# A two-block fp32 layer on one core: C's decays as a fourth score matmul, turned maxima, squares on ScalarE, and softmax visits in halves with other PSUM banks

## What is computed

```python
def forgetting_attention(q, k, v, logf):
    c = jnp.cumsum(logf, axis=1)
    ...
        s = jnp.einsum('bqhd,bkhd->bhqk', qblk, k).astype(jnp.float32) * scale
        decay = jnp.transpose(cblk, (0, 2, 1))[:, :, :, None] - c_k[:, :, None, :]
        s = jnp.where((dist >= 0)[None, None], s + decay, -jnp.inf)
        p = jax.nn.softmax(s, axis=-1)
        return jnp.einsum('bhqk,bkhd->bqhd', p.astype(v.dtype), v)
```

## Time and profile before

| | |
|---|---|
| median of 3 runs | 1279.6 us (1277.46 to 1279.94) |
| the profiled execution | 1279.9 us |
| its span, first to last instruction | 1278.1 us |
| TensorE matmuls busy | 1234.3 us, 97% |
| DVE / ScalarE / GpSimd busy | 658.9 / 550.4 / 659.0 us |
| transfers | 113.94 MB, mean 89 GB/s |
| chain of work that ended last | 83% TensorE, 9% DVE |

### The profile page before, as it was taken

The page is one execution under the profiler, slowest core; times in us unless marked ns, Lnnn a source line. Parts: engine busy times, 40 slices in busy tenths (PEclk is TensorE's granted clock), DMA queues, the critical chain, the costliest instruction groups (busy, mean ns, idle before and its releaser), DMA issues.

```text
span 1278.1 us, 17097 instructions
## 1 busy us (share of the span) xinstructions
PE 1234.3 (97%) x6230; PEld 982.5 (77%) x6230; DVE 658.9 (52%) x1217; ACT 550.4 (43%) x1066; POOL 659.0 (52%) x501
## 2 busy tenths in 40 slices
PE   7998989999999999999989999999999999999996
PEld 5886767777878888888776676878888888888885
DVE  6436744765743312125277545459999999200024
ACT  4544544676654333235552647542332333322344
POOL 4772223235346544446454464646767776655542
PEclk9998999999999999999988999999999999999998
DMA  5333222113222433343231121423333333433321
GB/s 197 112 113 98 67 61 73 50 50 83 67 66 83 114 92 91 95 152 112 82 84 50 42 71 53 116 82 84 99 99 99 90 92 87 128 96 94 100 74 66
DMA packets 63939, 113.94 MB, mean 89 GB/s; under 512 B 7016, under 2 KB 12776, under 8 KB 63856
## 3 DMA queue, kind: packets, MB, share of 16 engines
q1 hardware_dynamic: 63712, 112.84, 31.0%
q10 hardware_dynamic: 144, 0.00, 0.0%
HBM read 110.71 MB, written 2.11 MB: 88 GB/s over the span
## 4 chain that ended last, share of the span: by engine, by line
PE 83%; DVE 9%; ACT 3%; issue 2%; POOL 1%; DMA 1%; DVEq 0%; SPq 0%; ACTq 0%; POOLq 0%
PE pb L911 24%; PE pb L912 24%; PE pb L914 24%; PE pb L1065 2%; PE pb L1041 1%; DVE P L1774 1%; PE pb L1016 1%; POOL HL L2191 1%; DVE B L1644 1%; PE pb L979 1%; DVE U L1644 1%; DVE sq L1632 1%; PE pb L981 1%; PE pb L980 1%; POOL wlo L2191 1%
## 5 line engine op out<-in xcount | busy, mean ns | idle before, releaser
L2191 POOL TENSOR_TENSOR wlo<-raw,whi 128x512 fp32r<-128x512 f32 (+3 forms) x398 | 539.6, 1372 | 437.7 <-ACT whi L1247 437.5
L911 PE MATMUL pb<-HH,whi 128*128 128x512 f32 x968 | 391.4, 404 | 0.0
L912 PE MATMUL pb<-HL,whi 128*128 128x512 f32 x968 | 384.1, 397 | 0.0
L914 PE MATMUL pb<-HH,wlo 128*128 128x512 f32 x968 | 382.6, 395 | 0.0
L1247 ACT ACTIVATE whi<-raw 128x512 fp32r<-128x512 f32 (+3 forms) x398 | 233.2, 613 | 184.5 <-PE pb L914 156.5
L911 PEld LDWEIGHTS pb<-HH,whi 128*128 128x128 f32 x968 | 183.3, 189 | 47.0 <-issue 3.7
L914 PEld LDWEIGHTS pb<-HH,wlo 128*128 128x128 f32 x968 | 182.7, 189 | 42.6
L912 PEld LDWEIGHTS pb<-HL,whi 128*128 128x128 f32 x968 | 182.9, 189 | 42.2 <-issue 2.4
L1644 DVE SCALAR_TENSOR_TENSOR cv<-zf,vecs,cv 128x512 f32<-128x512 f32 x88 | 124.9, 1419 | 3.1
L1322 ACT ACTIVATE P<-P,stat 128x256 f32<-128x256 f32 (+3 forms) x96 | 51.1, 533 | 92.9 <-DVE stat L1639 68.9
L1635 DVE TENSOR_TENSOR X<-pb,X 128x512 f32<-128x512 f32 x24 | 16.6, 691 | 137.7 <-PE pb L914 137.3
(11 more groups left out here) (386 smaller groups left out, 1913.1 us busy)
## 6 DMA issues: line engine op xcount, KB each, us to landing
raw<-in_wall SPq DMA_DIRECT2D x362, 256.0 KB, 2.7
raw<-in_wall SPq DMA_DIRECT2D x16, 192.0 KB, 2.4
raw<-in_wall SPq DMA_DIRECT2D x8, 260.0 KB, 3.1
X<-in_xT SPq DMA_DIRECT2D x8, 256.0 KB, 5.3
N<-c_sums SPq DMA_DIRECT2D x8, 256.0 KB, 4.1
X<-in_xT SPq DMA_DIRECT2D x2, 1024.0 KB, 7.7
outT<-PP SPq DMA_DIRECT2D x8, 256.0 KB, 2.2
raw<-in_wall SPq DMA_DIRECT2D x12, 128.0 KB, 2.1
```

Of the source, the lines that this page charges most:

```text
L911: pe.do.matmul(b, hi, xh[k], start=start, stop=False)
L912: pe.do.matmul(b, hi, xl[k], start=False, stop=False)
L914: m = pe.do.matmul(b, lo, xh[k], start=False, stop=stop)
L2191: g.do.tensor_tensor(lo, x, hi.bitcast(F32), ALU.subtract).then_inc(*up(name, point))
```

## The change

1. C's decay is part of the scores. c and -c are split into high and low parts of 8 rows each (`decay`, in the middle of qC 3), and SP copies the rows one at a time into two operands: AQ with rows c_hi, c_lo, 1, 1 and AK with 1, 1, -c_hi, -c_lo, at partitions 0 to 3 for even heads and 64 to 67 for odd ones. GpSimd sets the ones at the start. `pair` has a fourth matmul over these four rows. The bias is now a constant mask DC; `cq`, the trip through memory and the broadcasts go.
2. The operation that adds the bias also multiplies by -1 and takes the minimum; the exponential has scale -1. C and A need no negation after it; B compares with the negated sink.
3. The squares of x in `first` are made on ScalarE; `lambda` comes after `columns1`; the low parts of odd tiles in `x_norm` are made on DVE.
4. A visit has two halves, after the 4th and the 8th step of a tile (after every step of vA): scores, values, turns and the first normalisation, then the second normalisation and the next biases.
5. Scores and turns have banks 4, 5, 6, 3, 2 (4, 5, 6 during vA as before), projection tiles 0 and 1.

```diff
-        banks = {"main": (0, 1, 2, 3), "first3": (0, 1, 2), "S": (), "Y": (7,), "m3": (0, 1, 2), "x5": (3, 4, 5, 6, 7),
+        banks = {"main": (0, 1, 2, 3), "first2": (0, 1), "S": (), "Y": (7,), "m3": (0, 1, 2), "x5": (3, 4, 5, 6, 7),
                  "x4": (3, 4), "all": (0, 1, 2, 3, 4, 5, 6, 7)}[ring]
         if ring == "S":
             banks = self.score_banks
-        if ring in ("S", "main", "first3"):
+        if ring in ("S", "main", "first2"):
...
-        if i == 7:
+        if i in (3, 7):
             self.step()
...
     def pipeline(self, groups):
 
+
...
-            if 0 < i <= n:
-                for u in groups[i - 1]:
-                    self.add("normal", *u)
...
-            for g in groups[i + 2:i + 4]:
-                for u in g:
-                    self.add("pre", *u)
...
                 self.turns(g)
-            if two:
-                for u in two[0]:
-                    self.add("normal", *u)
+            for u in two[0] if two else ():
+                self.add("normal", *u)
             if kind == "A" and i >= 6 and groups[i - 5][0][2] == 3:
                 h = groups[i - 5][0][1]
                 self.take("S", ("late", h))
                 self.add("late", h)
                 self.ready.add(("yA", h))
+            yield
+            if two:
+                for u in two[1]:
+                    self.add("normal", *u)
+                for g in groups[i + 2:i + 4]:
+                    for u in g:
+                        self.add("pre", *u)
             yield
 
     def turns(self, units):
...
             add("first", k)
             if k <= LOOK:
                 self.split_to(k)
...
-        add("lambda")
...
         add("columns1")
+        add("lambda")
...
-        self.tile("main", ("qC", 3))
+        self.tile("main", ("qC", 3), between=lambda i: add("decay") if i == 4 else None)
         add("out", "qC", 3)
-        take("S", ("cq",))
-        add("cq")
         c, a, b = softmax_units()
         self.background.append(self.pipeline(c))
         add("masks")
-        self.score_banks = (4, 5, 6, 3)
+        self.score_banks = (4, 5, 6, 3, 2)
...
         for k in range(KD):
             self.enter("win", k, VA)
             add("vA", k)
-            if k % 2:
-                self.step()
+            self.step()
...
-        ident, ones, bdones, maskC = (CST[:, 128 * i:128 * i + 128] for i in range(4))
-        DA, DB = CST[:, 512:1024], CST[:, 1024:1280]
+        ident, ones, bdones = (CST[:, 128 * i:128 * i + 128] for i in range(3))
+        DC, DA, DB = CST[:, 384:896], CST[:, 896:1408], CST[:, 1408:1664]
...
+        cum_hi, cum_lo, neg_hi, neg_lo = (like(f"cum{n}", n, dt=F32R)[0:8, :] for n in ("W1", "th1", "W2", "th2"))
+        AQ, AK = (tensor_at(f"decay_{n}", [P, 4 * T], F32R, place[n + "0"]) for n in ("vA", "qB"))
...
-            def forget_columns():
-                free(("cq",))
-                pe.wait_ge(*at("c"))
-                for m in range(4):
-                    i = pe.do.matmul(ps("cq")[:, 8 * m:8 * m + 8], cT[0:8, P * m:P * m + P], ident[0:8, 0:8],
-                                     start=True, stop=True)
-                i.then_inc(*up("small", ("full", ("cq",))))
-
             def pair(one, two):
...
                     for s in range(2):
                         rows = slice(64 * s, 64 * s + 64)
                         z = pe.do.matmul(ps(*tiles[s])[:, 0:wd], qs["q" + kind, t][rows, P * i:P * i + P],
-                                         ks["k" + kind, kt][rows, k0:k0 + wd], start=n == 0, stop=n == 2)
-                        if n == 2:
+                                         ks["k" + kind, kt][rows, k0:k0 + wd], start=n == 0,
+                                         stop=n == 2 and kind == "B")
+                        if n == 2 and kind == "B":
                             z.then_inc(*up("scored", ("full", tiles[s])))
+                if kind == "C":
+                    pe.wait_ge(*at("decay_in"))
+                    for s in range(2):
+                        rows = slice(64 * s, 64 * s + 4)
+                        pe.do.matmul(ps(*tiles[s])[:, 0:wd], AQ[rows, T * t + P * i:T * t + P * i + P],
+                                     AK[rows, T * t:T * t + wd], start=False, stop=True).then_inc(
+                            *up("scored", ("full", tiles[s])))
 
             def scores(kind, h, i):
                 if kind != "A":
...
                 a.do.activation(mh[k], xk[k], ACT.Copy, scale=vecs("norm_gain", k)).then_inc(*up("xhi", ("m_hi", k)))
+                if k > 2:
+                    a.wait_ge(*at("sq_step", k - 2))
+                a.do.activation(sqs[(k - 1) % 2] if k else acc, xk[k], ACT.Square).then_inc(*up("a_norm", ("sq", k)))
...
+            def decay():
+                a.wait_ge(*at("c"))
+                a.do.activation(cum_hi, cT[0:8, :], ACT.Copy).then_inc(*up("a_small", ("cum_hi",)))
+                a.do.activation(neg_hi, cT[0:8, :], ACT.Copy, scale=-1.0).then_inc(*up("a_small", ("neg_hi",)))
...
-                        a.wait_ge(*at("c_minus"))
+                        a.wait_ge(*at("c"))
...
-                    a.do.activation(p, p, ACT.Exp, bias=stat(u, 4 * m + 1), accum_out=stat(u, 4 * m + 2)).then_inc(
+                    a.do.activation(p, p, ACT.Exp, bias=stat(u, 4 * m + 1), scale=-1.0,
+                                    accum_out=stat(u, 4 * m + 2)).then_inc(
...
-                b = sqs[(k - 1) % 2] if k else acc
-                if k > 2:
-                    v.wait_ge(*last("v_sq"))
-                mul(b, xk[k], xk[k], name="v_sq")
-                v.wait_ge(*last("v_sq"))
                 if k:
-                    add(acc, acc, b, *[("sq_sum",)] * (k == KD - 1), name="v_sq")
+                    v.wait_ge(*at("sq", k))
+                    if k > 1:
+                        v.wait_ge(*last("v_sq"))
+                    add(acc, acc, sqs[(k - 1) % 2], ("sq_step", k), *[("sq_sum",)] * (k == KD - 1), name="v_sq")
 
...
+                for n in {2: (1,), 4: (3,), 6: (5,), 7: (7,)}.get(k, ()):
+                    v.wait_ge(*at("x_hi", n))
+                    v.do.tensor_tensor(hl[n], sqs[n % 2], hh[n].bitcast(F32), ALU.subtract).then_inc(
+                        *up("v_lo", ("x_lo", n)))
...
-                v.wait_ge(*last("v_small"))
-                affine(fx, cT[0:8, :], -1.0, None, ALU.mult, None, ("c_minus",))
...
+            def decay():
+                v.wait_ge(*at("cum_hi"))
+                v.wait_ge(*at("c"))
+                v.do.tensor_tensor(cum_lo, cT[0:8, :], cum_hi.bitcast(F32), ALU.subtract).then_inc(
+                    *up("v_lo", ("cum_lo",)))
+                v.wait_ge(*at("neg_hi"))
+                fused(neg_lo, cT[0:8, :], -1.0, neg_hi.bitcast(F32), ALU.mult, ALU.subtract, ("neg_lo",), name="v_lo")
...
             def scores(kind, h, i):
-                u, wd, n = (kind, h, i), width(kind, i), bias_of[kind, h, i]
-                bb = Br[n % 2]
+                u, wd = (kind, h, i), width(kind, i)
                 if kind == "C":
-                    cq = CQ[:, 8 * i + h:8 * i + h + 1]
-                    v.wait_ge(*at("neg", h))
-                    v.wait_ge(*at("cq"))
-                    if n == 0:
-                        v.wait_ge(*at("full", ("qC", 3)))
-                    fused(bb[:, P * i:P * i + P], Nr[h % 4][:, P * i:P * i + P], cq, maskC, ALU.add, ALU.add,
-                          *[("neg_used", h)] * (i == 3), name="v_soft")
-                    if i:
-                        affine(bb[:, 0:P * i], Nr[h % 4][:, 0:P * i], cq, None, ALU.add, None,
-                               *[("neg_used", h)] * (i == 3), name="v_soft")
-                    v.wait_ge(*last("v_soft"))
-                    bias = bb[:, 0:wd]
+                    bias = DC[:, 384 - P * i:512]
                 else:
+                    n = bias_of[kind, h, i]
                     v.wait_ge(*at("bias", n))
-                    bias = bb[:, 384 - P * i:512] if kind == "A" else bb[:, 256 - wd:256]
+                    bias = Br[n % 2][:, 384 - P * i:512] if kind == "A" else Br[n % 2][:, 256 - wd:256]
                 for m in range(2 if kind == "A" else 1):
                     s = soft[(*u, m)]
                     if s >= 6:
                         v.wait_ge(*at("p_used", s - 6))
                     v.wait_ge(*at("full", ("scores", *u, m)))
-                    v.do.tensor_tensor_reduce(Pr[s % 6][:, 0:wd], ps("scores", *u, m)[:, 0:wd], bias, 1.0, LOWEST,
-                                              ALU.add, ALU.max, stat(u, 4 * m)).then_inc(
-                        *up("v_soft", ("empty", ("scores", *u, m))))
-                    v.wait_ge(*last("v_soft"))
+                    most = ("most", u, m)
+                    v.do.tensor_tensor_reduce(Pr[s % 6][:, 0:wd], ps("scores", *u, m)[:, 0:wd], bias, -1.0, -LOWEST,
+                                              ALU.add, ALU.min, stat(u, 0 if kind == "B" else 4 * m + 1)).then_inc(
```

(43 more changed lines are left out.)

37 lines of the change are left out of this document (16 added, 21 removed).

## The result

The changed kernel takes 1284.3 us (median of 5 runs, 1282.6 to 1284.8), the kernel before 1278.9 (5 runs, 1277.5 to 1279.9). The ratio is 1.0040, 95% interval 1.0025 to 1.0054: **slower by 0.4%**, where 1274.9 us was forecast and 1262 to 1283 was the range. The profiled execution took 1284.8 us with a span of 1283.0, so it stands 4.9 us of span above the one before (1278.1).

The account below looks back on a forecast made before the run. TensorE, busy for 97% of the span, was taken as the bound. Gains of -23.6 us and costs of +18.6 gave -5.0 against the profiled 1279.9: 1274.9 us forecast, range 1262 to 1283.

Parts of the forecast that it names:

- C's waits: TensorE's 14 waits in C's stage, 12.8 us, go except two in the visit during vA: -10.7 us.
- four small issues in a row take 1.78 us, 0.445 each: SP's queue: 32 single-row DMAs at this pace, the last leaving at 102.9, stall TensorE by +11.8 us.
- Rival (e): SP's 32 transfers hold one another up; at 0.8 us apiece 1285.9 us, slower from about 0.6; chance 0.07.
- the start: Up to norm1: lambda behind `columns1` and squares on ScalarE remove TensorE's lost time, net -4.9 us.
- Rival (b): The start isn't gained: squares delay ScalarE's splits until TensorE waits as before; 1279.8 us, chance 0.09.
- the odd x_lo: Four low parts go from GpSimd to DVE where TensorE waits for neither: 0 us.
- cq: The `cq` matmuls, which take TensorE from 84.82 to 85.90, go: -1.1 us.
- the old low clock: After TensorE's longest wait, half of 3.85 us at the lower clock until 115.3 is no longer lost: -1.9 us.
- The fourth matmul: C's visits: sixteen pairs stream for 2.5 us, three shape changes in each of 8 visits cost 2.4: +4.9 us.
- The low clock: Behind the new stall at the first four-row matmul the clock drops as after the earlier long wait: +1.9 us.
- A and B: TensorE's waits in the stages of A and B go: -4.3 and -0.7 us.
- Two projection banks: Projection tiles in two banks: one is needed again only after another tile of 5.6 us and a visit: 0 us.

Follow-up runs that it names:

- the run with two queues: Changed kernel with its 32 single-row DMAs kept, AK's 16 issued by ScalarE and AQ's 16 by SP: 1272.5 us, ratio 0.9957.
- the execution with eight DMAs: Changed kernel with AQ and AK filled by 8 DMAs of four rows into one, instead of 32 of one row: 1265.3 us, ratio 0.9887.
- the run with 64 rows: Kernel with 8 DMAs, its fourth matmul contracting over 64 rows (AQ zero beyond its four), memsets at norm1: 1262.5 us, ratio 0.9871.
- the one with the maxima turned back: Kernel with 8 DMAs, but maximum, wait, negation as before the change, in all three stages: 1267.6 us, ratio 0.9919.
- the third set: Third of three sets of follow-up runs, each comparing kernels with the kernel before on the same chip; its median there 1278.1 us.

## Why the prediction was wrong, step by step

The main mechanism was right: an exchange of C's waits against one stall behind SP's queue. Two steps failed. The time is 9.9 us of span above the sum; they make 5.3 and 4.4 of it, and neither alone would have left the range.

**The first step that failed is "four small issues in a row take 1.78 us, 0.445 each".** The rows from which it came are DMAs out of memory, of one row to 128 partitions; the new ones go out of SBUF into a single partition and cost 0.63 an issue, with one source row or four. Which of the two differences makes it dearer no run separates (out of SBUF into memory, -c took one issue of 0.35 in the kernel before). So the last issue leaves at 108.7 and not 102.9, 5.8 us later; the landing took 0.8 less than the 2.6 assumed, TensorE was there 0.3 sooner, and the stall is 17.1 for 11.8. Rival (e) named the point, 0.6 us apiece, from which the kernel is slower than before, and it was passed; its cause, transfers that hold one another up, is ruled out by the run with two queues. With the measured stall in its place the prediction's own sum gives 1280.2: most of what is missing from there is the second step.

**The second is the start**, which was to bring 4.9 and keep it. It brought 4.3 at norm1 (5.5 in the execution with eight DMAs, whose start is the same), and 0.5 at the first sums matmul. The prediction followed TensorE's gain no further than norm1: it had no term for what stands behind x_norm in ScalarE's program, vC's evictions, whose pace did not change. Rival (b) has nearly the size, but not the cause: no wait for ScalarE's splits came back. That the odd x_lo cost nothing was right, by the run that undid them.

**cq**: -1.1 predicted; kA's first tile comes 1.5 us earlier where the first sums matmul came 0.5 earlier, so -1.1.

**C's waits** -10.7, **the old low clock** -1.9: between kA's first tile and the first visit of A, at the same place in the order of projections, the changed kernel loses 12.0 us. Stall 17.1, clock 2.1 and the fourth matmul 6.4 are 25.6; so the waits and the old low clock gave 13.6 where 12.6 were forecast. Right in sum, though this is a remainder and not a measurement, and not by the reason given first: the fifth bank did little of it, so the agreement is in part luck.

**The fourth matmul** +4.9: 6.4. The streaming of 2.5 was right (in the run with 64 rows a pair is followed after 0.11 to 0.12 us at 128 and 256 columns, 0.17 at 384 and 0.24 at 512). The changes of shape cost 3.9 over the eight visits, not 2.4: 0.12 at four places of each, where 0.10 at three was forecast. The rows had changes between 128 and 64 only, and the change back to 128 was taken as no dearer than before. The Trainium skill (TensorEngine Tiling (Array Packing), Key Properties) says that a change of tiling mode drains TensorE. The trace fits that, at 0.24 us for the two sides of one pair.

**The low clock** behind the stall +1.9: 2.1. Right. In the execution with eight DMAs it comes after 2.1 us of waiting as well.

**A and B** -5.0: the visits between the first of A and the end of attention give 5.5 (the changed kernel is 10.5 us behind at the first visit of A, 5.0 at the end of attention, each at the same place among the projections). Right. Two projection banks at 0: right, for no wait on one appears.

The sum by what was measured: -0.5 - 1.1 + 12.0 - 5.5 = +4.9, as in the spans (where 5.0 was forecast the other way: 9.9 apart = 5.3 for the stall, 4.4 for the start, 1.5 for the fourth matmul, 0.2 for the clock, less 1.0 and 0.5 for the waits). After the attention the difference stays within 1 us: 5.0 at its end, 4.2 behind the second block's low clock, 4.9 at the last instruction.

## What to carry to other kernels

Price a DMA by its issue on the queue that carries it, taken from a DMA of the same kind, and count issues before bytes: 32 small ones on a path are 20 us here, and folding four rows into one issue took 15 us off the wait. When a wait is removed early, ask what the next engine in line has queued ahead of the work that TensorE now wants sooner; a gain ends at the first step whose pace didn't change. And an operand padded with zeros to its neighbours' shape can cost less than the change of shape, if the memsets find an engine that is idle.

## What the runs showed that I had not expected

- An issue of a DMA out of SBUF into one partition of SBUF holds SP or ScalarE for 0.57 to 0.61 us (0.62 to 0.63 with the gap; one of 0.72 among the eight), with 1 or 4 source rows, against 0.33 for a weight load and 0.445 for a row sent to 128 partitions. Two queues at once keep that pace each.
- GpSimd's memset of 4 x 2048 takes 1.83 us, as that of 128 x 2048 does (1.82): here the rows are free.
- Whether the lower clock follows a short wait differs between executions in which the wait is the same. The decays' wait of 2.1 us was followed by 3.4 us of it in the kernel with eight DMAs and by none in the one with the maxima turned back; vC's wait of 2.7 us by none with eight DMAs (1.00 from 70 to 74 us) and by 3.4 us in the changed kernel (0.5 from 70.3 to 73.7).
- In the second block, where the same two waits stand in every kernel, the lower clock takes up to 3.3 us more in one execution than in another. Executions of one kernel differ likewise: the kernel before, in the third set, ran from 1275.2 us at a mean clock of 0.992 to 1280.1 at 0.986. So of the comparisons with the eight DMAs above, those of 1.8 to 3.4 us rest on the places in the trace, and only those of 7 us and more stand clear of this by the times alone.
